# Diffusion backbone step: the first norm deferred, and the opening's loads and products taken k tile by k tile

## What is computed

```python
def modulation(cond, w_mod, b_mod):
    m = jax.nn.silu(cond) @ w_mod + b_mod
    return m.reshape(cond.shape[0], 1, N_MOD, D_MODEL)

def modulate(x, g, shift, scale):
    return rms_norm(x, g) * (1.0 + scale) + shift

def swiglu(h, w_in, w_out):
    g, u = jnp.split(h @ w_in, 2, axis=-1)
    return (jax.nn.silu(g) * u) @ w_out
...
    x = x + m[2] * (0.5 * swiglu(modulate(x, norm_g[0], m[0], m[1]), w_in[0], w_out[0]))
```

## Time and profile before

| | us |
|---|---|
| median of 3 runs | 1518.71 (1517.93 to 1518.75) |
| the profiled execution | 1518.2 |
| its span in the trace | 1515.8 |
| PE busy | 1508.3 (100%) |
| DVE busy | 1087.1 (72%) |
| ACT busy | 668.1 (44%) |

### The profile page before, as it was taken

The page is one execution under the profiler, slowest core; times in us unless marked ns, Lnnn a source line. Parts: engine busy times, 40 slices in busy tenths (PEclk is TensorE's granted clock), DMA queues, the critical chain, the costliest instruction groups (busy, mean ns, idle before and its releaser), DMA issues.

```text
span 1515.8 us, 22012 instructions
## 1 busy us (share of the span) xinstructions
PE 1508.3 (100%) x8886; PEld 1446.7 (95%) x8886; DVE 1087.1 (72%) x1747; ACT 668.1 (44%) x1031; POOL 34.8 (2%) x45
## 2 busy tenths in 40 slices
PE   9999999999999999999999999999999999999999
PEld 5999999988889999999999999999997899999999
DVE  5887887789887887876678787877578876343332
ACT  5433333254686633333363333325458765333221
POOL 0000000000031000000000000000020000000000
PEclk9999999999999999999999999999999999999999
DMA  9756566543233365655455655654331033333233
GB/s 391 280 211 233 207 247 223 188 153 116 94 98 139 126 232 201 241 195 184 165 186 190 227 214 213 231 185 152 116 124 57 3 137 112 139 113 137 100 131 118
DMA packets 52276, 258.00 MB, mean 170 GB/s; under 512 B 6608, under 2 KB 8912, under 8 KB 37072
## 3 DMA queue, kind: packets, MB, share of 16 engines
q1 hardware_dynamic: 49632, 253.13, 46.2%
q10 hardware_dynamic: 2544, 3.48, 0.7%
HBM read 253.29 MB, written 3.29 MB: 169 GB/s over the span
## 4 chain that ended last, share of the span: by engine, by line
PE 96%; DVE 1%; DMA 1%; ACT 1%; issue 1%; SPq 0%; DVEq 0%; ACTq 0%
PE ps L2178 30%; PE ps L2180 29%; PE ps L2179 29%; PE ps L2830 1%; DMA wm_first<-in_w_mod_first 1%; PE ps L2721 1%; PE ps L2839 1%; PE ps L2853 1%; PE ps L2576 1%; PE ps L2545 1%; PE ps L2287 0%; PE ps L2505 0%; PE ps L2310 0%; PE ps L2563 0%; PE ps L2228 0%
## 5 line engine op out<-in xcount | busy, mean ns | idle before, releaser
L1375 DVE TENSOR_TENSOR w_lo<-w_raw,w_hi 128x2048 fp32r<-128x2048 f32 (+3 forms) x177 | 347.3, 1964 | 233.8 <-ACT w_hi L799 231.5
L2178 PE MATMUL ps<-hx_hi,w_hi 128*128 128x384 f32 (+1 forms) x1432 | 480.2, 335 | 0.0
L2179 PE MATMUL ps<-hx_lo,w_hi 128*128 128x384 f32 (+1 forms) x1432 | 478.6, 334 | 0.0
L2180 PE MATMUL ps<-hx_hi,w_lo 128*128 128x384 f32 (+1 forms) x1432 | 478.5, 334 | 0.0
L799 ACT ACTIVATE w_hi<-w_raw 128x2048 fp32r<-128x2048 f32 (+3 forms) x177 | 292.7, 1654 | 407.1 <-DMA w_raw<-in_w_out 210.7
L2178 PEld LDWEIGHTS ps<-hx_hi,w_hi 128*128 128x128 f32 x1432 | 268.9, 188 | 2.3 <-issue 1.8
L2179 PEld LDWEIGHTS ps<-hx_lo,w_hi 128*128 128x128 f32 x1432 | 268.9, 188 | 0.0
L2180 PEld LDWEIGHTS ps<-hx_hi,w_lo 128*128 128x128 f32 x1432 | 268.8, 188 | 0.0
L2180 PE MATMUL ps<-g_hi,w_lo 128*128 128x384 f32 x704 | 236.6, 336 | 0.0
L2178 PE MATMUL ps<-g_hi,w_hi 128*128 128x384 f32 x704 | 236.5, 336 | 0.0
L2179 PE MATMUL ps<-g_lo,w_hi 128*128 128x384 f32 x704 | 236.5, 336 | 0.0
(11 more groups left out here) (293 smaller groups left out, 1501.3 us busy)
## 6 DMA issues: line engine op xcount, KB each, us to landing
w_raw<-in_w_in SPq DMA_DIRECT2D x88, 1024.0 KB, 4.8
wm<-in_w_mod SPq DMA_DIRECT2D x128, 512.0 KB, 5.7
w_raw<-in_w_out SPq DMA_DIRECT2D x64, 704.0 KB, 4.1
w_raw<-in_w_qkv SPq DMA_DIRECT2D x12, 1024.0 KB, 4.8
wm_first<-in_w_mod_first SPq DMA_DIRECT2D x8, 1024.0 KB, 19.0
w_raw<-in_w_o SPq DMA_DIRECT2D x7, 1024.0 KB, 4.8
w_raw<-in_w_qup SPq DMA_DIRECT2D x8, 576.0 KB, 3.7
w_raw<-in_w_down SPq DMA_DIRECT2D x6, 704.0 KB, 4.0
```

The costliest lines, as they stand in the source:

```text
L1375: nc.vector.tensor_tensor(w_lo[:, slot, 0:width], w_raw[:, slot, 0:width], w_hi[:, slot, 0:width].bitcast(F32), ALU.subtract).then_inc(w_l ...
L2178: nc.tensor.matmul(out, l_hi, r_hi, start=first, stop=False)
L2179: nc.tensor.matmul(out, l_hi, r_lo, start=False, stop=False)
L2180: return nc.tensor.matmul(out, l_lo, r_hi, start=False, stop=last)
```

## The change

The first FFN's norm (n = 0) is deferred too. Panels 0 and 1 multiply xg (k = 0, 1 raw in a new buffer xg_raw with plain products, k = 2 to 7 split in hx_hi and hx_lo) with two shift columns, and their outputs are scaled afterwards (scale_out, first_panels). Sum of squares and broadcast move behind the products of k = 3 and the rows of k = 5. Panels 0 and 1 and x are loaded in pieces: w_in is stored k tile by k tile, and a quarter holds two k tiles of both panels; wm_first 0 is the first large load. The rounding of w follows by quarters. h for panel 2 on is made between and behind (to_tile, to_high, scaled, h_low). The five wm tiles are asked for after panel 3, mod units start at m = 3 with 3 or 4 per panel instead of 3 from m = 0, the parameter loads wait for the last h_lo and stand behind first_panels. The other FFNs change only in tile numbers. Cut to its core, with new lines mainly (the old order is printed above):

```diff
-        return {0: 3, 1: 3 if m > 2 else 0, 2: 3 if m > 2 else 0, 3: 0}[f]
+        return {0: (3 if m % 2 else 4) if m > 2 else 0, 1: 3 if m > 2 else 0, 2: 3 if m > 2 else 0, 3: 0}[f]
...
+
+            def load_first(k):
                 sp.dma_start(wm_first[:, k], d["w_mod_first"][k]).then_inc(wmf_loaded[k], 16)
...
+
+            def load_x(ks, signal):
+                sp.dma_start(x[:, ks, :], d["xT"][:, ks, :]).then_inc(signal, 16)
+
+            def load_quarter(q):
+                sp.dma_start(w_raw[:, 0:2, quarter(q)],
+                             d["w_in"][0][0:2].rearrange("m p c -> p m c")[:, :, quarter(q)]).then_inc(first_in[q], 16)
+
+            load_first(0)
+            load_x(slice(0, 2), first_in[0])
+            load_quarter(0)
+            load_first(1)
+            load_first(2)
+            load_x(slice(2, 4), first_in[1])
+            load_quarter(1)
+            load_first(3)
+            load_x(slice(4, KD), x_in)
+            load_first(4)
+            load_quarter(2)
+            load_first(5)
+            load_first(6)
+            load_quarter(3)
+            load_first(7)
...
-                    while asked < MODS and (MOD_AT[asked] <= n + 3 or asked < FIRST_MODS + WM_SLOTS) and (
+                    while n >= SLOTS and asked < MODS and (MOD_AT[asked] <= n + 3 or asked < FIRST_MODS + WM_SLOTS) and (
...
+                def xg_first(k):
+                    if k == 0:
+                        act.wait_ge(first_in[0], 32)
+                    act.wait_ge(gains, 2 * k + 2)
+                    out = xg_raw[:, k, :] if k < RAW else hx_hi[:, k, :]
+                    nc.scalar.activation(out[:, T:T + 2], modc[:, k, :], ACT.Copy)
+                    for s, seg in SEGS:
+                        ins = nc.scalar.activation(out[:, seg], x[:, k, seg], ACT.Copy, scale=gmul[:, k, s:s + 1])
+                    ins.then_inc(xg_hi_done, 1)
+
+                def first_high(q):
+                    for m in range(2):
+                        if m == 0:
+                            act.wait_ge(first_in[q], 32 if q < 2 else 16)
+                        nc.scalar.activation(w_hi[:, m, quarter(q)], w_raw[:, m, quarter(q)], ACT.Copy).then_inc(
+                            w_hi_done if q == 3 else half_hi, 1)
 
                 def to_tile(k):
                     latents(0, k, gmul[:, k, 1:2], modc[:, k, 1:2])
+                    if k % 2 == 0:
+                        contexts(0, k, gmul[:, k, 0:1], modc[:, k, 0:1])
+
+                def to_high(k):
+                    if k < KD - 1:
+                        act.wait_ge(xg_used, xg_uses(0, k))
+                    else:
+                        act.wait_ge(panel_used, 2)
+                    h_high(0, k)
 
                 copied(0)
...
+                xg_first(0)
+                square(0)
+                square(1)
+                copied(1)
+                xg_first(1)
+                copied(2)
+                square(2)
+                square(3)
+                first_high(1)
+                xg_first(2)
+                copied(3)
+                square(4)
+                square(5)
+                xg_first(3)
+                square(6)
+                square(7)
+                copied(4)
+                first_high(2)
+                xg_first(4)
                 act.wait_ge(bc_ready, 1)
                 nc.scalar.activation(sqacc[:], ps[:, 6, 0:T], ACT.Copy).then_inc(rb_ready, 1)
+                copied(5)
                 to_tile(0)
...
+                xg_first(5)
+                to_high(0)
                 to_tile(1)
...
+                copied(6)
+                first_high(3)
+                xg_first(6)
+                to_high(1)
                 to_tile(2)
...
+                copied(7)
+                to_high(2)
+                to_tile(3)
+                xg_first(7)
+                to_high(3)
...
+                    if k == 5:
+                        high_half(3, 0)
+                high_half(3, 1)
+                act.wait_ge(cond_in, 16)
+                nc.scalar.activation(cond[:], cond[:], ACT.Silu).then_inc(cond_ready, 1)
+                first_panels(0, 0)
...
+            act.wait_ge(h_lo_done, h_val(0, KD - 1))
             for dst, name in ((ropes, "ropes"), (gq, "gq"), (gm, "gm"), (gmT, "gmT"), (subg, "subg"), (gdown, "gdown"),
                               (lamp, "lamp")):
                 act.dma_start(dst[:] if name != "lamp" else dst, d[name]).then_inc(params_in, 16)
...
+            ffn_in(0, 2)
...
+                def first_low(q):
+                    for m in range(2):
+                        if q == 3:
+                            v.wait_ge(w_hi_done, m + 1)
+                        else:
+                            v.wait_ge(half_hi, 2 * (q - 1) + m + 1)
+                        nc.vector.tensor_tensor(w_lo[:, m, quarter(q)], w_raw[:, m, quarter(q)],
+                                                w_hi[:, m, quarter(q)].bitcast(F32), ALU.subtract).then_inc(
+                                                    w_lo_done if q == 3 else half_lo, 1)
+
+                def first_xg_low(k):
+                    v.wait_ge(xg_hi_done, xg_val(0, k))
+                    nc.vector.tensor_tensor(hx_lo[:, k, T:T + 2], modc[:, k, :], hx_hi[:, k, T:T + 2].bitcast(F32),
+                                            ALU.subtract)
+                    xg_low(0, k)
+
+                v.wait_ge(small_in, 32)
                 gains_of(0)
...
+                add(1)
+                gains_of(1)
+                add(2)
+                add(3)
+                gains_of(2)
+                first_low(1)
+                first_xg_low(2)
+                gains_of(3)
+                add(4)
+                add(5)
+                first_xg_low(3)
+                add(6)
+                add(7)
+                gains_of(4)
+                invert(0)
+                first_low(2)
+                first_xg_low(4)
                 scaled(0, 0)
...
                 scaled(0, 1)
...
+                gains_of(5)
                 context(0, 1, 0)
+                first_xg_low(5)
                 scaled(0, 2)
                 h_low(0, 0)
+                gains_of(6)
+                first_low(3)
+                first_xg_low(6)
                 scaled(0, 3)
...
                 h_low(0, 1)
+                context(0, 3, 0)
+                gains_of(7)
                 h_low(0, 2)
...
+                scaled(0, 4)
+                first_xg_low(7)
+                scaled(0, 5)
+                context(0, 5, 0)
                 low_half(2, 0)
+                h_low(0, 3)
                 low_half(2, 1)
+                scaled(0, 6)
+                h_low(0, 4)
+                scaled(0, 7)
+                context(0, 7, 0)
+                h_low(0, 5)
+                scale_out(0, 0, 0)
+                h_low(0, 6)
+                low_half(3, 0)
+                h_low(0, 7)
+                low_half(3, 1)
+                scale_out(0, 0, 1)
+                first_panels(0)
...
                     def plain(m, k, half):
+                        if half == 0 and m == 0:
+                            pe.wait_ge(xg_hi_done, xg_val(0, k))
+                            if k == 0:
+                                pe.wait_ge(first_in[0], 32)
+                        t = 2 * k + half
+                        mm = nc.tensor.matmul(ps[:, bank_pair(m) + half, 0:T + 2], w_raw[:, m, t * P:(t + 1) * P],
+                                              xg_raw[:, k, 0:T + 2], start=k == 0, stop=False)
+                        if m == 1 and half:
+                            mm.then_inc(xg_used, 1)
...
+                    zeros(3)
                     pe.wait_ge(condT_ready, 1)
...
+                    pe.wait_ge(dve_consts, 4)
                     mod_rows(0)
...
+                    zeros(1)
                     mod_columns(0)
...
+                    zeros(2)
+                    plain(0, 0, 0)
+                    plain(0, 0, 1)
+                    plain(1, 0, 0)
                     mod_rows(1)
...
+                    plain(1, 0, 1)
                     mod_columns(1)
...
                     mod_rows(2)
                     plain(0, 1, 0)
+                    plain(0, 1, 1)
                     mod_columns(2)
...
                     plain(1, 1, 0)
+                    plain(1, 1, 1)
                     mod_rows(3)
...
                     tile(0, 2, 0)
                     tile(0, 2, 1)
+                    mod_columns(3)
                     tile(1, 2, 0)
                     tile(1, 2, 1)
                     mod_rows(4)
                     tile(0, 3, 0)
                     mod_columns(4)
                     tile(0, 3, 1)
+                    sum_squares(0)
+                    tile(1, 3, 0)
+                    tile(1, 3, 1)
                     mod_rows(5)
...
+                    pe.wait_ge(gains, 7)
+                    broadcast(0)
+                    tile(0, 4, 0)
+                    tile(0, 4, 1)
                     mod_columns(5)
...
```

(78 more changed lines are left out.)

175 lines of the change are left out of this document (57 added, 118 removed).

## The result

The median went from 1518.37 us (1517.93 to 1518.75) to 1522.96 us (1521.38 to 1524.95), nine runs of each on one chip: a ratio of 1.0029 [1.0019, 1.0039], 4.6 us slower. The forecast was 1519.4, its range ended at 1522.3. The profiled execution of after took 1522.96, with a span of 1521.0: 5.2 us more than before's 1515.8, of which 0.4 is not in the times (2.0 us lie around this span, 2.4 around before's).

What follows compares the result with a forecast made beforehand. PE's own stream bounds the kernel, so only panel 4's start against 61.76 counts: -2.7 (panel 1) + 1.6 (panel 2) - 0.05 - 0.1 + 1.75 (panel 4) = +0.5, plus 0.2 for pieces: +0.7, 1519.4 us; range 1516.4 to 1522.3.

Steps and rivals of the forecast that it cites:

- First product 10.2: Opening on PE: the first real product starts at 10.2 instead of 16.47, 6.2 us sooner.
- Rival C: Opening: PE's clock rises late, slowing rows, zeros and plain products; +1.2 to +3.5 us on the forecast, chance 0.11.
- Landings: Opening transfers: wm_first 4 lands at 22.9, the last at 33.6 as now; smaller pieces cost 0.2 us.
- X = 39.3: Panel 1 on ACT: X, the end of xg_first(7), comes at 39.3, with ACT the tightest engine.
- Panel 1's end at X + 2.95, 42.2: PE, after DVE's xg_low(7) and four tiles: panel 1 ends at 42.2, 2.7 us sooner than 44.95.
- the prediction's floor: PE work without waits: first product 10.2 + 29.6 + 1.4 puts panel 1's end at 41.2 at the earliest.
- Panel 2 at X + 4.5: Panel 2's w_lo on DVE is ready at 43.8, PE having run out at 42.2; gives back 1.6 us.
- w_lo of panel 4 at X + 22.9: ACT's chain with seven DMA issues (3.3 us), high(4), then low(4): panel 4's w_lo ready at 62.2.
- PE's wait there, 1.75: Before panel 4, PE could start at 60.45 but waits 1.75 us for w_lo.
- Rival D: load(3) takes 7.0 us instead of 4.7 with five wm loads right behind it; 1521.7 to 1522.7, chance 0.12.
- the forecast's +0.7: Whole run: the summed change against the kernel before, +0.5 us plus 0.2 for the pieces.

Runs made afterwards that it cites:

- e6: e4 with panel 3's w_hi halves on ACT (and w_lo halves on DVE) moved behind h of k = 6 and 7: 1519.47 us, ratio 1.0007.
- e4: Changed kernel with the edits of e1 and e3, sum of squares ahead of k = 3's last product, broadcast ahead of rows 5: 1518.82 us, ratio 1.0005.
- e7: Kernel before with panels 0 and 1 loaded in four column pieces each and x in four: 1519.70 us, ratio 1.0008.
- e12: Kernel before with panels 0 and 1 each in four loads of 256 KB, 2 KB per row, x as it was: 1519.24 us, ratio 1.0007.
- e10: e9 with panels 0 and 1 in two loads of 1 MB instead of four of 0.5 MB: 1518.72 us, ratio 1.0003.
- e1: Changed kernel with ACT's seven parameter DMA issues moved into the middle of the FFN (m = 8, behind the silu): 1518.79 us, ratio 1.0003.
- e8: Changed kernel with only panel 3's w_hi and w_lo halves moved behind h of k = 6 and 7: 1520.02 us, ratio 1.0011.
- e2: Changed kernel with four zero matmuls on PE between panel 3's end and the wait for panel 4's w_lo: 1521.76 us, ratio 1.0025.
- e3: Changed kernel with panel 2's w_hi halves ahead of to_high(3) on ACT and w_lo halves ahead of h_low(3) on DVE: 1523.04 us, ratio 1.0029.
- e9: e6 with load(4) asked for ahead of the five wm loads instead of behind them: 1517.65 us, ratio 0.9998.

## Why the prediction was wrong, point by point

- **First product 10.2**: 10.69. wm_first 0 landed at 6.2 (forecast 6.6), but its rows took 1.63 us, not 1.07: its matmuls took up to 636 ns, later ones 379. I read that as the lower clock, though the granted clock prints 1.00 there. Rival C came true for half a us, and even that was swallowed: in e6 the rows took 1.07, in e4 1.54, and panel 2 starts at 45.13 and 45.12.
- **Landings**, the step that failed first. Forecast 0.2 us for the pieces; wm_first 4 landed at 24.6 instead of 22.9, the last at 34.7 instead of 33.6. Of the 1.7 at wm_first 4, 0.7 is a slip of the forecast: by its own rule, before's landing at 26.1 less 1 MB at 0.42 MB/us, it lands at 23.6. The other 1.0, as the 1.1 at the last, goes to the pieces, give or take the 0.5 by which equal openings differ. Before, issue and landing of wm_first 4:

```profile
L666 SPq DMA_DIRECT2D wm_first<-in_w_mod_first x1: 432/432/432, 5.7 to 5.7; - x1
...
DMA to landing us min/median/max: 20.4/20.4/20.4
```

  I took 404 GB/s of the earlier trace rows as the price of small loads, a stretch in which nobody waits for one transfer among the others. In e7 and e12 four loads for one cost 1.7 and 2.1 us. The Trainium skill (DMA: Bandwidth & Descriptors, "Measured (HBM→SBUF, 128 partitions, SWDGE, issued from GpSimd)") asks for 1 MiB per DMA, from which the prediction estimated 2 us and set it aside; its size fits e12 and is twice that of after, and that I set it aside was wrong. e10, with 1 MB pieces, was no faster, though: which bytes stand ahead counts as well.
- **X = 39.3**: 41.12. From wm_first 4 to X the forecast had 16.4 us and the trace 16.5. That was right in size; in cause it wasn't: I had ACT as the tightest and nearly without idle from 29 to 39. It waited 2.94 us for the broadcast and 0.40 for the last gain, and e4 shows that its part can end sooner without moving X. Nor did the rows of tile 7 stand right behind their landing: wm_first 7 came at 34.7, PE reached them at 37.12.
- **Panel 1's end at X + 2.95, 42.2**: 44.4, X + 3.3. With the first product where it was, the prediction's floor is 10.69 + 29.6 + 1.4 = 41.7. The 2.7 on top are three waits that the timeline names (0.38, 0.94 and 0.55 us) and short gaps; the forecast had 1.0.
- **Panel 2 at X + 4.5**: 45.62 = 41.12 + 4.5. The sum is exact, partly by luck: panel 1 ended 0.35 later behind X than forecast, and PE waited 1.2 and not 1.6.
- **w_lo of panel 4 at X + 22.9**: X + 24.4. The stall stood where the prediction put it, on the engine and behind the instructions that it named (e1, e8). Mis-sized were the issues, 4.2 us instead of 3.3, and what lies ahead of them, 0.5, with load(3) 0.4 later than forecast.
- **PE's wait there, 1.75**: 2.75. And one term was left out of the sum altogether: a wait of that length costs the clock. e2 puts 1.4 us on it, and e8 1.5. The prediction had looked at the clock only at the start (rival C). With the wait as it was and the clock kept, e2 came to 1521.76, inside the forecast's range.
- **Rival D** (load(3) at 7.0) was not what happened: it took 4.8. Its neighbour load(4) took 10.6 behind the wm loads, against a forecast landing of 54.7; in after it came at 57.1 and was just hidden, in e6 it was the bound.

The sum: X 1.8 later than forecast, w_lo 1.5 later behind it, less the 0.2 that the pieces were given already, and 1.4 of clock make 4.5; the forecast's +0.7 and 4.5 are the 5.2 of the spans.

What stays open: why 0.4 us less lie around the span where wm_first 0 is loaded first, why some of the seven issues took twice as long in after as in before, and how much of the pieces' price is their number and how much the length of their rows in after itself. None of these was tried.

## What to carry to other kernels

Before an order is changed on an engine that also issues DMAs, find what hides each issue now; seven issues in a place with cover were free (e1), and in one without it they cost 4.2 us of the run. A stall of PE has a second price when the clock falls behind it, here 1.4 to 1.6 us for the stalls of 2.4 and 2.8 us and nothing for the one of 1.35; a forecast stall between these should carry it as a term of its own. A load split for an earlier start delays those behind it: the saving at the front of a full queue was 5.8 us here, and at the first panel that PE runs without a stop nothing of it was left. And a transfer's landing is best forecast from the same transfer's landing in the trace of before: by that, wm_first 4 would have been forecast 0.7 us later and nearer.

## What the runs showed of the hardware

- A DMA issue on ACT's queue holds ACT, and its length isn't fixed: in before six of the seven took 0.45 us each, 3.2 us in all; in after gmT took 0.88 and gdown 0.93, 4.2 in all; in e3 3.9 in all; in e8 subg took 1.22, 4.5 in all.
- The granted clock fell to 0.50, the level of 1.2 GHz, after PE had waited 2.75 us (after) or 2.43 (e3), and not after 1.35 (e8) or 0.79 (e6). Nothing between 1.35 and 2.43 was measured. In e3 three passes ran at the full clock before it fell, and it was back some 3 us later. After 1.35 us with nothing, as after 2.9 us with zeros (e2), it cost nothing. This busy time by stretch of e3 stands against that of after:

```profile
64.00:66.00 2.00, 0.41 (x2) 0.41 (x3) 2.00 (x2) 0.00 (x0) 0.00 (x0) 1.00 0.88 274
66.00:68.00 2.00, 2.00 (x9) 2.00 (x8) 0.56 (x2) 1.96 (x2) 0.00 (x0) 0.58 0.61 250
68.00:70.00 2.00, 2.00 (x8) 2.00 (x8) 1.61 (x1) 0.74 (x2) 0.00 (x0) 0.57 0.00 0
```

- With the same bytes, loads in rows of 2 KB ran at 412 GB/s in 10 to 20 us, four loads for one at 397 to 399, whole ones at 425.
- A load waits for those ahead of it in the queue: load(3) took 4.8 us with nothing ahead (after), load(4) 10.6 (after) and 11.9 (e6) behind five loads of 0.5 MB, and 6.4 in e9 with one load ahead.
